# An output projection with the norm of its rows set between half products, and the next stage's first context product moved to its end

## The chip, the core and the metric

The kernel runs on one core of a Trainium2 chip. The metric is the device time of one execution in microseconds (us). The kernel's engines each follow a program of their own and meet at semaphores: TensorE (PE, with its weight loads as PEld), VectorE (DVE), ScalarE (ACT), GpSimd (POOL) and the sync engine (SP), which here only issues transfers.

## The reference, cut to what matters

The reference is a chain of two blocks in float32. The first ends in an attention layer, whose output is multiplied by `b_w_out`, gated and added to `x`. The second block starts with a layer (`layer = 0`) on the 1024 rows of `x` and on 256 context rows:

```python
h_lat = rms_norm(x_lat, norm1_g[layer]) * (1 + m_lat[1]) + m_lat[0]
h_ctx = rms_norm(x_ctx, norm1_g[layer]) * (1 + m_ctx[1]) + m_ctx[0]
...
z_lat = h_lat @ w_in
z_ctx = h_ctx @ (w_in if need_ctx else w_in[:, :EVEN_CTX_COLS])
...
q_ctx = z_ctx[..., EVEN_CTX_COLS:EVEN_CTX_COLS + A_Q_W].reshape(bsz, n_ctx, A_KV_HEADS, g, A_HEAD_DIM)
s_ctx = spatial_gating(z_ctx[..., EVEN_CTX_COLS + A_Q_W:], sgu_norm_g, sgu_w, sgu_b)
```

`w_in` is 1024 by 1792, and comes as four tiles of 1024 by 512 (the third padded): Q (the queries), V (the half of the gated part that is normed), K (keys and values) and U (the other half).

## The kernel before, in words

The kernel is a chain of stages (`block_...`). Each stage has one program for each engine; at its end all engines meet at a barrier. Activations stay in on-chip memory, as `X` (ten tiles of 128 rows by 1024, eight of `x` and two of the context) and `hT` (the normed rows, transposed, in eight pieces of 128 by 1280). Weights come from DRAM in tiles of 2 MB (`load_w`, issued by SP) into a ring of three slots. `slot_of` (L84) says which tile goes to which slot, and `next_tile` which tile is loaded into a slot once its present tile is used up. From the KV stage to the first layer's end only slots 1 and 0 hold weights; slot 2 holds sums of weights (`w_sums`).

**`block_out`** (L1886), as the stage `bout`, computes `x = x + gate * (attention output @ b_w_out)` and the transposed norm of all ten row tiles. TensorE's work is 16 half products: row tile i (0 to 7) by column half t (0, 1), each 8 matmuls of 128x512 (`product`, L399; the profile records each float32 matmul twice, so 16 records), into four PSUM banks (2 to 5) in turn. `gate_rows` (L1094) brings the gate into banks 6 and 7, once. For each half VectorE runs `residual_add` (L1236, L1238).

**`Follow`** (L265) is the norm. Its list of tiles is here `[8, 9, 0, ..., 7]`: the two context tiles come first (they are the `lead` of 2), so follow tile n holds row tile n-2. For each tile:

- ScalarE: `squares` (L285, sum of squares), then `normed` (root L298, scaled copy L302) into one of two buffers `xn`. `squares` of tile n writes into buffer n % 2 and so waits until tile n-2 has been transposed (`free`).
- VectorE: `dve_var` (L318) after the squares, `dve_rst` (L323) after the root.
- TensorE: `pe`, eight transposes (L351), four into bank 0 and four into bank 1. It waits for `normed` of this tile, and until both banks have been emptied of the tile before (`placed`).
- VectorE empties bank 0 (`dve_tile`, L332) and ScalarE bank 1 (`act_tile`, L311) into `hT`.

What sets the order is the list `turns`: after which row tile's products which follow tiles are transposed. It is `[[], [0], [1, 2], [3, 4], [5], [6], [7], [8]]`, and tile 9 comes after the loop. On VectorE `dve_tile` of `turns[i]` stands behind both `residual_add` of row tile i, and `dve_var(i + 2)`, which waits for ScalarE, stands behind that and ahead of the next `residual_add`.

SP loads the context rows (`in_ctx`, L1925) at the start, stores each finished row tile, and loads the next stage's tiles Q and V at the end (L1933 and L200).

**`block_ein`** (L2057) is the next stage. It starts with the products of the two context tiles by the Q tile (`rows_of_tile`, 16 matmuls of 128x512, into banks 0 and 1), which VectorE scales and copies (L2418). Then come 12 `Quads`, blocks of a product made with fewer multiplications, for which VectorE first makes sums of rows (`quad_sums`, L537 to L540, four times) and of weights (L522, L523, L529, L530). Quads 0 to 3 use tile Q, 4 to 7 tile V, 8 to 11 tile U. Each opens with two products (`pe_open`); the third waits for VectorE's `dve_11` (L482). At quad 4 the products of the context rows by the V tile are put in (16 matmuls again), and ScalarE's gelu of them. Then follow the K tile's products and the rest. VectorE makes the sums of row blocks 2 and 3 after the two copies of L2418.

Of the kernel before, what the change touches and what calls it, by code (L numbers as in the profile page):

```python
# [25 lines left out]
P = 128  # L26
# [58 lines left out]
def slot_of(n):  # L85
# [10 lines left out]
    own, one, two = [(2, 1, 0)[(k + j) % RING] for j in range(RING)]  # L96
# [1789 lines left out]
def block_out(cr, name, w0, nt, gates, tiles, col, router=None, homes=(A_OT, A_H), gated=None):  # L1886
# [28 lines left out]
    turns = [[], [0], [1, 2], [3, 4]] + [[i + 1] for i in range(4, nt)] if lead else [[i - 1] if i else [] for i in range(nt)]  # L1915
# [5 lines left out]
    with nc.Block() as block:  # L1921
        @block.sync
        def _(sp):
            if lead:
                sp.dma_start(Xr[:, NT:NTC], io["ctx"].rearrange("b (i p) d -> (b p) i d", p=P)).then_inc(x_in, 16)  # L1925
            if router is not None:
                sp.dma_start(rw, io["router"][:, router]).then_inc(r_in, 16)
            for i in range(nt):
                if i == nt - 1:
# [14 lines left out]
        def _(pe):  # L1944
# [12 lines left out]

            for i in range(nt):
# [10 lines left out]
                for n in turns[i]:  # L1969
                    fol.pe(pe, n)  # L1970
# [11 lines left out]
        def _(act):  # L1982
# [12 lines left out]
            for i in range(nt):  # L1995
                for n in turns[i]:
# [12 lines left out]
        def _(dve):  # L2009
# [7 lines left out]
            for i in range(nt):  # L2017
# [3 lines left out]
                for n in turns[i]:  # L2021
                    fol.dve_tile(dve, n)
# [9 lines left out]
def block_bout(cr):  # L2032
    block_out(cr, "bout", W_BOUT, NT, [(MC_B + 16, V_C)], [NT, NT + 1] + list(range(NT)), MC_L)
# [23 lines left out]
def block_ein(cr):  # L2057
# [23 lines left out]
    S, T = x_sums(cr), w_sums(cr)  # L2081
# [40 lines left out]
    with nc.Block() as block:  # L2122
        @block.sync
        def _(sp):
# [6 lines left out]
            sp.wait_ge(uc.full, 4 + NTC)  # L2131
# [32 lines left out]
        def _(pe):  # L2164
# [56 lines left out]
            cr.wait_w(pe, W_Q)  # L2221
            for i in (8, 9):
                rows_of_tile(cr.w(W_Q), i, 512)
# [21 lines left out]
        def _(act):  # L2245
# [19 lines left out]

            for n in range(9):
                if n < 8:
                    qd.act_1(act, n, blocks(n)[0])
                if n == 4:
                    for r in range(2):  # L2270
                        act.wait_ge(uc.full, 3 + r)
                        gelu(vr[:, 8 + r], uc.bank(2 + r)).then_inc(uc.empty, 1)
# [24 lines left out]
            act.wait_ge(uc.empty, 4 + NTC)  # L2297
            for m in range(4):
                act.wait_ge(uc.full, 4 + NTC + m + 1)
# [1338 lines left out]
```

## Time and profile before

| what | value |
|---|---|
| three runs | 4673.64, 4674.6, 4679.7 us, median 4674.6 us |
| the profiled execution | 4671.94 us, of which the span from the first to the last instruction is 4670.2 us |
| mean granted TensorE clock | 0.964 |
| stage `bout` | from 1430.8 to 1570.0 us of the span |
| stage `ein` | from 1570.9 to about 1822 us |
| TensorE busy | 4343.9 us, 93% of the span |

The span is cut into stages by their first instruction; times within it are microseconds from its start. A timeline row gives the start, the length, the engine, the line, the operation with its output and input, the count, and in brackets the engine's idle time before it with what ended it. Matmul records overlap a little (each runs on for a while after the next has started), so the pace is read from start to start. PEclk is the share of full clock granted.

### The profile page before, as it was taken

The numbers are of one execution on the slowest core, as the hardware profiler recorded it, in microseconds if no ns is written. First come the engines' busy times: TensorE is split into PE (matmuls) and PEld (weight loads), VectorE is DVE, ScalarE is ACT, GpSimd is POOL, SyncE is SP. The second block draws the span as 40 slices with busy tenths as digits, with TensorE's granted clock in tenths as the row PEclk, the third lists the DMA queues.
The fourth block names the chain that finished last, engine by engine and source line by source line (L and its number), as shares of the span: only waits on it lengthen the run. The fifth ranks groups of instructions, "written<-read, shape, count | busy, mean of one in ns | idle before, by whom it ended". The sixth has DMA issues, their size and how long they took to land. (4 is left out here: it accounts for less than half of the span.)

```text
span 4670.2 us, 63663 instructions
## 1 busy us (share of the span) xinstructions
PE 4343.9 (93%) x25960; PEld 3116.2 (67%) x25960; DVE 1648.0 (35%) x4208; ACT 1007.1 (22%) x2270; POOL 230.0 (5%) x281
## 2 busy tenths in 40 slices
PE   7996899999999999996999999989999995999996
PEld 3444446888664587643888888869656644888885
DVE  5408234433783344725111111133445524111111
ACT  2011122112663123722100000021135521000001
POOL 0100000000220000000000001000000000000000
PEclk8998999999999999997999999999999997999998
DMA  7668211223420112115677777741161013888887
GB/s 282 228 107 315 95 46 39 92 84 111 169 83 28 61 59 91 49 63 200 233 260 256 258 256 251 267 145 41 66 209 37 1 55 114 314 312 318 320 310 259
DMA packets 132953, 756.89 MB, mean 162 GB/s; under 512 B 13729, under 2 KB 52385, under 8 KB 97297
## 3 DMA queue, kind: packets, MB, share of 16 engines
q1 hardware_dynamic: 107248, 669.78, 39.1%
q0 software_dynamic: 20272, 64.76, 5.1%
q10 hardware_dynamic: 5232, 19.63, 1.2%
q8 instruction: 132, 2.16, 0.2%
q14 instruction: 69, 0.56, 0.0%
HBM read 663.46 MB, written 91.19 MB: 162 GB/s over the span
## 5 line engine op out<-in xcount | busy, mean ns | idle before, releaser
L2828 PEld LDWEIGHTS psum<-arena,w_ring 128*128 128x128 f32 x8192 | 1022.6, 192 | 15.5 <-issue 15.5
L2828 PE MATMUL psum<-arena,w_ring 128*128 128x160 f32 (+1 forms) x8192 | 1027.0, 288 | 4.5 <-ACT arena L2910 3.0
L399 PE MATMUL psum<-w_ring,arena 128*128 128x512 f32 (+3 forms) x1608 | 635.0, 553 | 13.0 <-PEq L194 9.6
L399 PEld LDWEIGHTS psum<-w_ring,arena 128*128 128x128 f32 x1608 | 305.0, 193 | 311.5 <-issue 282.4
L2843 PE MATMUL psum<-w_ring,arena 128*128 128x512 f32 x1024 | 450.0, 592 | 0.0
L427 PE MATMUL psum<-w_ring,arena 128*128 128x256 f32 (+1 forms) x2016 | 435.6, 377 | 15.3 <-PEq L194 7.1
L427 PEld LDWEIGHTS psum<-w_ring,arena 128*128 128x128 f32 x2016 | 377.8, 192 | 66.8 <-issue 17.6
L2969 DVE TENSOR_TENSOR arena<-arena,psum 128x320 f32<-128x320 f32 (+1 forms) x128 | 58.2, 455 | 956.9 <-PE psum L2828 956.9
L399 PE MATMUL psum<-arena,w_ring 128*128 128x512 f32 (+1 forms) x880 | 373.3, 580 | 2.8 <-DVE arena L332 1.6
L2894 ACT ACTIVATE arena<-psum 128x320 f32<-128x320 f32 (+1 forms) x128 | 52.5, 410 | 1311.0 <-PE psum L2828 1311.0
L2843 PEld LDWEIGHTS psum<-w_ring,arena 128*128 128x128 f32 x1024 | 189.7, 190 | 214.9 <-issue 214.9
L1683 PE MATMUL psum<-arena 64*128 64x256 f32 (+5 forms) x1056 | 319.8, 526 | 12.4 <-PEq L194 11.0
L427 PE MATMUL psum<-arena,w_ring 128*128 128x256 f32 x1344 | 295.7, 380 | 5.0 <-DVE arena L482 3.5
L399 PEld LDWEIGHTS psum<-arena,w_ring 128*128 128x128 f32 x880 | 165.5, 192 | 190.1 <-issue 186.2
L427 PEld LDWEIGHTS psum<-arena,w_ring 128*128 128x128 f32 x1344 | 253.4, 190 | 41.1 <-DVE w_ring L523 3.6
L1696 PEld LDWEIGHTS psum<-consts,arena 128*128 128x128 f32 x1552 | 172.9, 141 | 122.4 <-issue 68.7
L1733 ACT ACTIVATE arena<-psum 128x512 f32<-128x512 f32 (+3 forms) x436 | 194.2, 482 | 271.9 <-PE psum L1696 261.6
L1741 ACT ACTIVATE arena<-arena,small 128x640 f32<-128x640 f32 (+8 forms) x272 | 244.6, 900 | 6.0 <-DVE small L1788 5.9
L1696 PE MATMUL psum<-consts,arena 128*128 128x128 f32 x1552 | 224.0, 279 | 5.9 <-ACT arena L1741 4.5
L1713 PE MATMUL psum<-arena 128*64 128x128 f32 x3104 | 225.5, 281 | 0.0
L1683 PEld LDWEIGHTS psum<-arena 64*128 64x128 f32 (+1 forms) x1056 | 126.2, 191 | 100.4 <-issue 73.2
L1713 PEld LDWEIGHTS psum<-arena 128*64 128x64 f32 x3104 | 164.2, 136 | 42.5 <-issue 41.4
(378 smaller groups left out, 3427.4 us busy)
## 6 DMA issues: line engine op xcount, KB each, us to landing
w_ring<-in_wstream SPq DMA_DIRECT2D x258, 2048.0 KB, 7.8
x_rows<-arena SPq DMA_DIRECT2D x26, 512.0 KB, 2.7
w_ring<-in_wstream ACTq DMA_DIRECT2D x6, 2048.0 KB, 7.8
xn_rows<-arena POOLq DMA_DIRECT2D x18, 512.0 KB, 2.9
arena<-f_rows SPq DMA_DIRECT2D x8, 1024.0 KB, 7.6
arena<-x_rows SPq DMA_DIRECT2D x2, 4096.0 KB, 21.3
arena<-x_rows SPq DMA_DIRECT2D x8, 1024.0 KB, 9.5
arena<-in_x_first SPq DMA_DIRECT2D x4, 1024.0 KB, 21.9
```

The costliest lines, as they stand in the source:

```text
L399: last = cr.nc.tensor.matmul(bank_ap, l, r, start=(k == 0), stop=(k == len(pairs) - 1))
L427: last = self.cr.nc.tensor.matmul(out, l, r, start=(start and k == 0), stop=(k == len(pairs) - 1), skip_group_check=True)
L1683: nc.tensor.matmul(cr.bank[2 * h + C % 2][:, 0:p.b - p.a], s_.q(h), p.keys(h), start=True, stop=True).then_inc(qk, 1)
L1696: last = nc.tensor.transpose(cr.bank[4 + h][:, n * P:(n + 1) * P], s_buf[:, s % 3, h, col:col + P], cr.const(C_ID))
L1713: last = nc.tensor.matmul(o[h * HD:(h + 1) * HD], s_.pv[blk][1](h), t_buf[:, h, G % 2, n * P:(n + 1) * P], start=(blk == 0), stop=(blk == ...
L1733: copy = lambda to, of: nc.scalar.activation(to, of, ACT.Copy)
L1741: nc.scalar.activation(v, v, ACT.Exp, bias=shift_of(s, h), scale=-1.0, accum_out=rsum[:, s % 3, h:h + 1]).then_inc(pr, 1)
L2828: last = nc.tensor.matmul(half(bank0 + v)[:, c], w[:, k, m * P:(m + 1) * P], xT[:, k, :], start=(k == 0), stop=(k == KT - 1))
L2843: last = nc.tensor.matmul(cr.bank[YB[h]][:, :], hid[:, k, 0:CAP], w[:, k, :], start=(k == 0), stop=(k == KT - 1))
L2894: nc.scalar.activation(sa[:, v % 2], half(v % 2), ACT.Silu).then_inc(a_e, 1)
L2969: nc.vector.tensor_tensor(hid[:, 2 * v:2 * v + 2], sa[:, v % 2], half(2 + v % 2), ALU.mult).then_inc(b_e, 1)
```

## The change

It has four parts.

1. In `block_out`, `turns` now goes by half products: for `bout` tile 0 is transposed after half 2 (row tile 1, first half), tile 1 after half 3, tile 2 after half 4, tile 3 after half 5, tile 4 after half 7, and from there one tile after each second half, as before. VectorE's `dve_tile` stands at the same places. The other stages that use `block_out` keep their order.
2. The two products of context tiles by tile Q move from the start of `ein` to the end of `bout` (`following`): the first between the transposes of tiles 8 and 9, the second behind those of tile 9, into banks 6 and 7. VectorE's last act in `bout` is a wait for the second. In `ein` it copies from banks 6 and 7 without a wait.
3. In `ein` the products of the context rows by tile V move from quad 4 to the stage's start, and ScalarE's gelu of them with them. The unit numbers fall by two.
4. The ring: tile Q goes to slot 2 and is loaded at the start of `bout`, ahead of the context rows; in `ein` the weight sums are in slot 1; tile K goes to slot 2. Later tiles have slots 1 and 2 exchanged. The load of tile Q at the end of `bout` is gone; that of tile V stays.

```diff
@@ slot_of
+    if n < W_EIN:
+        return (1, 0)[(n - W_KV) % 2]
     if n < W_MOD2:
-        return (1, 0)[(n - W_KV) % 2]
+        return (2, 0)[(n - W_EIN) % 2]
     if n < W_OIN:
-        return (2, 1, 0)[(n - W_MOD2) % RING]
+        return (1, 2, 0)[(n - W_MOD2) % RING]
...
@@ block_out
-    turns = [[], [0], [1, 2], [3, 4]] + [[i + 1] for i in range(4, nt)] if lead else [[i - 1] if i else [] for i in range(nt)]
+    turns = {2: [0], 3: [1], 4: [2], 5: [3]} if lead else {3: [0], 5: [1]}
+    turns.update({2 * i + 1: [i - 1 + lead] for i in range(3, nt)})
+    of_half = lambda s: turns.get(s, ())
+    f_ok, = cr.sems(name, "following_rows")
...
         def _(sp):
+            if follower is not None:
+                cr.load_w(sp, follower)
             if lead:
                 sp.dma_start(Xr[:, NT:NTC], io["ctx"]...
...
-                if i == nt - 1:
+                if i == nt - 1 and follower is None:
                     sp.wait_ge(un.full, 2 * nt - 1)
                     cr.load_w(sp, cr.next_tile(w0))
...
+            def following(r):
+                w = cr.w(follower)
+                for k in range(KT):
+                    last = nc.tensor.matmul(cr.bank[6 + r][:, :], hT[:, k, (NT + r) * P:(NT + r + 1) * P], w[:, k, :], start=(k == 0), stop=(k == KT - 1))
+                return last
...
+            if follower is not None:
+                cr.wait_w(pe, follower)
+                pe.wait_ge(g_ok, 2)
+                following(0)
             fol.pe(pe, len(tiles) - 1)
+            if follower is not None:
+                following(1).then_inc(f_ok, 1)
...
             fol.dve_tile(dve, len(tiles) - 1)
+            if follower is not None:
+                dve.wait_ge(f_ok, 1)
@@ block_ein
-    S, T = x_sums(cr), w_sums(cr)
+    S, T = x_sums(cr), w_sums(cr, 1)
...
-                            if n == 4:
-                                for i in (8, 9):
-                                    rows_of_tile(cr.w(W_V), i, 512)
...
-            cr.wait_w(pe, W_Q)
+            cr.wait_w(pe, W_V)
             for i in (8, 9):
-                rows_of_tile(cr.w(W_Q), i, 512)
+                rows_of_tile(cr.w(W_V), i, 512)
             quads(0, 8)
...
+            for r in range(2):
+                act.wait_ge(uc.full, r + 1)
+                gelu(vr[:, 8 + r], uc.bank(r)).then_inc(uc.empty, 1)
...
             for r in range(2):
-                dve.wait_ge(uc.full, r + 1)
-                ts(rawq[:, 8 + r], uc.bank(r), HD ** -0.5, None, ALU.mult).then_inc(uc.empty, 1)
+                ts(rawq[:, 8 + r], cr.bank[6 + r][:, :], HD ** -0.5, None, ALU.mult)
```

The rows below are the program's order on an engine: a line number, the operation, output and input, shape, and a count. In the changed kernel the same helper stands two lines further down (L353 is L351, L401 is L399).

TensorE from the second half product of `bout` on, before:

```order
L399 MATMUL psum<-w_ring,arena 128x512 x24
L351 MATMUL psum<-consts,arena 128x128 x8
L399 MATMUL psum<-w_ring,arena 128x512 x16
L351 MATMUL psum<-consts,arena 128x128 x16
L399 MATMUL psum<-w_ring,arena 128x512 x16
L351 MATMUL psum<-consts,arena 128x128 x16
L399 MATMUL psum<-w_ring,arena 128x512 x16
```

and in the changed kernel:

```order
L401 MATMUL psum<-w_ring,arena 128x512 x16
L353 MATMUL psum<-consts,arena 128x128 x8
L401 MATMUL psum<-w_ring,arena 128x512 x8
L353 MATMUL psum<-consts,arena 128x128 x8
L401 MATMUL psum<-w_ring,arena 128x512 x8
L353 MATMUL psum<-consts,arena 128x128 x8
L401 MATMUL psum<-w_ring,arena 128x512 x8
L353 MATMUL psum<-consts,arena 128x128 x8
L401 MATMUL psum<-w_ring,arena 128x512 x16
```

Before, two tiles were transposed directly behind one another twice (the x16 of L351); now a half product (x8 of L401) stands between any two of the first four.

VectorE from `dve_var` of tile 2 on, before (L1236 and L1238 are a residual add, L332 empties bank 0):

```order
L318 TENSOR_SCALAR small<-small 128x1
L323 RECIPROCAL small<-small 128x1
L1236 TENSOR_TENSOR arena<-psum,arena 128x512
L1238 TENSOR_TENSOR arena<-arena 128x512
L1236 TENSOR_TENSOR arena<-psum,arena 128x512
L1238 TENSOR_TENSOR arena<-arena 128x512
L332 TENSOR_SCALAR arena<-psum,gs,modcol 128x128 x4
L318 TENSOR_SCALAR small<-small 128x1
L323 RECIPROCAL small<-small 128x1
```

and in the changed kernel:

```order
L320 TENSOR_SCALAR small<-small 128x1
L325 RECIPROCAL small<-small 128x1
L1238 TENSOR_TENSOR arena<-psum,arena 128x512
L1240 TENSOR_TENSOR arena<-arena 128x512
L334 TENSOR_SCALAR arena<-psum,gs,modcol 128x128 x4
L1238 TENSOR_TENSOR arena<-psum,arena 128x512
L1240 TENSOR_TENSOR arena<-arena 128x512
L334 TENSOR_SCALAR arena<-psum,gs,modcol 128x128 x4
L320 TENSOR_SCALAR small<-small 128x1
L325 RECIPROCAL small<-small 128x1
```

Tile 0 is now placed between the two residual adds of row tile 1, and tile 1 behind the second.

TensorE from the last two half products of `bout` to the first quads of `ein`, before (the branches are the stage boundary):

```order
L399 MATMUL psum<-w_ring,arena 128x512 x16
L351 MATMUL psum<-consts,arena 128x128 x16
L1921 UNCONDITIONAL_BRANCH
L2163 UNCONDITIONAL_BRANCH
L399 MATMUL psum<-w_ring,arena 128x512 x16
```

and in the changed kernel:

```order
L401 MATMUL psum<-w_ring,arena 128x512 x16
L353 MATMUL psum<-consts,arena 128x128 x8
L1969 MATMUL psum<-w_ring,arena 128x512 x8
L353 MATMUL psum<-consts,arena 128x128 x8
L1969 MATMUL psum<-w_ring,arena 128x512 x8
L1926 UNCONDITIONAL_BRANCH
L2185 UNCONDITIONAL_BRANCH
L401 MATMUL psum<-w_ring,arena 128x512 x16
```

The two products of L1969 now stand in `bout`; the x16 behind the boundary are by tile V instead of tile Q, and the x16 that stood at quad 4 are gone from there.

## Rows read from the trace of the kernel before

**Rows 1.** the page's first lines.

```profile
span 4670.2 us, 63663 instructions
```

**Rows 2.** TensorE in time, output and context stages (start, length, idle before and its releaser).

```profile
1430.85 7.11 PE L399 MATMUL psum<-w_ring,arena 128*128 128x512 f32 x16 [2.78 <-PEq L194]
...
1474.79 1.04 PE L351 MATMUL psum<-consts,arena 128*128 128x128 f32 x8
1481.89 1.94 PE L351 MATMUL psum<-consts,arena 128*128 128x128 f32 x8 [6.06 <-DVE arena L332]
1483.62 15.99 PE L399 MATMUL psum<-w_ring,arena 128*128 128x512 f32 x32
...
1502.57 1.06 PE L351 MATMUL psum<-consts,arena 128*128 128x128 f32 x8 [2.08 <-DVE arena L332]
...
1517.20 1.04 PE L351 MATMUL psum<-consts,arena 128*128 128x128 f32 x8
1518.07 13.90 PE L399 MATMUL psum<-w_ring,arena 128*128 128x512 f32 x32
...
1561.03 1.04 PE L351 MATMUL psum<-consts,arena 128*128 128x128 f32 x8
1566.50 1.97 PE L351 MATMUL psum<-consts,arena 128*128 128x128 f32 x8 [4.43 <-ACT arena L302]
1570.92 16.78 PE L399 MATMUL psum<-w_ring,arena 128*128 128x512 f32 x32 [2.45 <-PEq L194]
1587.53 3.62 PE L427 MATMUL psum<-w_ring,arena 128*128 128x256 f32 x16
```

**Rows 3.** granted TensorE clock (PEclk) in three stretches.

```profile
1481.90:1488.00 6.10, 6.10 (x14) 3.54 (x15) 1.69 (x6) 3.68 (x8) 0.00 (x0) 0.51 0.11 45
...
1570.90:1577.00 6.10, 6.08 (x8) 2.70 (x9) 5.95 (x8) 0.00 (x0) 0.00 (x0) 0.53 0.42 131
...
1594.20:1598.00 3.80, 3.79 (x11) 3.16 (x12) 2.22 (x2) 0.00 (x0) 0.00 (x0) 0.62 0.00 0
```

**Rows 4.** ScalarE and VectorE in time, output stage.

```profile
1440.75 1.06 ACT L285 ACTIVATE arena<-arena 128x1024 f32<-128x1024 f32 x1
...
1475.93 1.06 ACT L285 ACTIVATE arena<-arena 128x1024 f32<-128x1024 f32 x1 [10.27 <-PE psum L351]
...
1480.38 1.36 DVE L332 TENSOR_SCALAR arena<-psum,gs,modcol 128x128 f32<-128x128 f32 x4
```

**Rows 5.** the sync queue, ScalarE and VectorE in time, around the stage's end.

```profile
1563.12 0.42 SPq L200 DMA_DIRECT2D w_ring<-in_wstream  x1
...
1568.50 1.50 ACT L311 ACTIVATE arena<-psum,modcol,gs 128x128 f32<-128x128 f32 x4 [2.06 <-PE psum L351]
...
1593.65 0.42 DVE L482 TENSOR_TENSOR arena<-arena,psum 128x256 f32<-128x256 f32 x1
```

**Rows 6.** TensorE in time, inside the next stage.

```profile
1594.21 41.35 PE L427 MATMUL psum<-w_ring,arena 128*128 128x256 f32 x184 [3.06 <-DVE arena L482]
1635.40 13.90 PE L399 MATMUL psum<-w_ring,arena 128*128 128x512 f32 x32
1649.13 27.79 PE L427 MATMUL psum<-w_ring,arena 128*128 128x256 f32 x128
...
1773.10 41.68 PE L427 MATMUL psum<-arena,w_ring 128*128 128x256 f32 x192 [0.68 <-DVE arena L482]
...
1822.42 5.66 PE L1683 MATMUL psum<-arena 64*128 64x256 f32 x20 [3.45 <-PEq L194]
```

**Rows 7.** VectorE in time, the weight sums of the V tile.

```profile
1637.29 1.23 DVE L523 TENSOR_TENSOR w_ring<-w_ring 128x1024 f32<-128x1024 f32 x1
```

**Rows 8.** DMA issues over the whole span: size, median to landing.

```profile
arena<-x_rows SPq DMA_DIRECT2D x2, 4096.0 KB, 21.3
...
arena<-in_ctx SPq DMA_DIRECT2D x1, 1024.0 KB, 5.1
```

**Rows 9.** landing of the weight tiles loaded from the sync queue.

```profile
DMA to landing us min/median/max: 7.4/7.8/30.2
```

More of the change, by code:

```diff
@@ L90, in slot_of @@
         return (2, 0, 1)[(n - W_MOD1) % RING]
+    if n < W_EIN:
+        return (1, 0)[(n - W_KV) % 2]
     if n < W_MOD2:
-        return (1, 0)[(n - W_KV) % 2]
+        return (2, 0)[(n - W_EIN) % 2]
     if n < W_OIN:
-        return (2, 1, 0)[(n - W_MOD2) % RING]
+        return (1, 2, 0)[(n - W_MOD2) % RING]
     k = (W_OIN - W_MOD2) % RING
-    own, one, two = [(2, 1, 0)[(k + j) % RING] for j in range(RING)]
+    own, one, two = [(1, 2, 0)[(k + j) % RING] for j in range(RING)]
     if n < W_MOE1:
@@ L1883, with block_out @@
 A_H = 20480
-def block_out(cr, name, w0, nt, gates, tiles, col, router=None, homes=(A_OT, A_H), gated=None):
+def block_out(cr, name, w0, nt, gates, tiles, col, router=None, homes=(A_OT, A_H), gated=None, follower=None):
     nc, io = cr.nc, cr.io
@@ L1968, in _ @@
                         gate_rows(cr, diag[:, t], (6, 7), g_mm)
-                for n in turns[i]:
-                    fol.pe(pe, n)
+                    for n in of_half(2 * i + t):
+                        fol.pe(pe, n)
                 for g in range(len(groups)):
@@ L1995, in _ @@
             for i in range(nt):
-                for n in turns[i]:
+                for n in (*of_half(2 * i), *of_half(2 * i + 1)):
                     fol.act_tile(act, n)
@@ L2020, in _ @@
                                  Xr[:, i, t * 512:(t + 1) * 512], fol.fin if t else None)
-                for n in turns[i]:
-                    fol.dve_tile(dve, n)
+                    for n in of_half(2 * i + t):
+                        fol.dve_tile(dve, n)
                 fol.dve_var(dve, i + lead)
@@ L2032, in block_bout @@
 def block_bout(cr):
-    block_out(cr, "bout", W_BOUT, NT, [(MC_B + 16, V_C)], [NT, NT + 1] + list(range(NT)), MC_L)
+    block_out(cr, "bout", W_BOUT, NT, [(MC_B + 16, V_C)], [NT, NT + 1] + list(range(NT)), MC_L, follower=W_EIN)
 def variant(lat, ctx):
@@ L2130, in _ @@
             cr.load_w(sp, cr.next_tile(W_V))
-            sp.wait_ge(uc.full, 4 + NTC)
+            sp.wait_ge(uc.full, 2 + NTC)
             cr.load_w(sp, cr.next_tile(W_K))
@@ L2268, in _ @@
                     qd.act_1(act, n, blocks(n)[0])
[L2269 to L2272, printed above, removed]
                 if n:
@@ L2296, in _ @@
             act.wait_ge(placed, NQ)
-            act.wait_ge(uc.empty, 4 + NTC)
+            act.wait_ge(uc.empty, 2 + NTC)
             for m in range(4):
-                act.wait_ge(uc.full, 4 + NTC + m + 1)
-                gelu(uT[:, m, SEQ:NTOK], uc.bank(4 + NTC + m)[:, 0:256]).then_inc(uc.empty, 1)
+                act.wait_ge(uc.full, 2 + NTC + m + 1)
+                gelu(uT[:, m, SEQ:NTOK], uc.bank(2 + NTC + m)[:, 0:256]).then_inc(uc.empty, 1)
             for n in range(8, 13):
@@ L2350, in rows_kv @@
             def rows_kv(i):
-                u = 4 + i
+                u = 2 + i
                 dve.wait_ge(uc.full, u + 1)
@@ L2382, in moments @@
                     else:
-                        dve.wait_ge(uc.empty, 3 + r)
+                        dve.wait_ge(uc.empty, 1 + r)
                     ln(nc.vector.bn_stats(bn6, vr[:, ROWS[r]]))
@@ L2480, in _ @@
                 if n == 8:
-                    dve.wait_ge(uc.full, 4 + NTC + 4)
+                    dve.wait_ge(uc.full, 2 + NTC + 4)
                     sums_34(2)
@@ L2486, in _ @@
                     dve.wait_ge(s_mx, 10)
[L2487 removed]
+                    dve.wait_ge(uc.empty, 2 + NTC + 4)
                     u = uT[:, :, SEQ:NTOK].rearrange("p g (i c) -> p g i c", c=P)
```

1 line of the change is left out of this document (removed).

## The prediction

> **What bounds the kernel now.** I read the page's head first: a span of 4670.2 us [rows 1], with TensorE busy nearly all of it. A stage is therefore worth what TensorE loses in it, and I next read TensorE in time through the two stages that the change touches, looking only at the brackets (idle time and its releaser) and at starts that come later than the pace allows. The pace is 6.87 us for a half product and 0.87 us for a tile's eight transposes: from 1517.20 to 1518.07 are the transposes, and 32 records (two half products) from 1635.40 to 1649.13 take 13.73 us [rows 2, 6]. Against that pace TensorE loses time at four places.
>
> - Before tile 2's transposes it waits 6.06 us for L332 on VectorE, and then works slowly: 1.94 us where the next tiles take 1.04, and 15.99 us where 32 records else take 13.90 [rows 2]. The granted clock there is 0.51, the lower level of 1.2 GHz [rows 3].
> - Before tile 4's transposes it waits 2.08 us, again for L332 [rows 2]. The transposes behind it take 1.06 us, so the clock did not fall.
> - At the end of `bout` it waits 4.43 us for the scaled copy of tile 9, transposes slowly, waits 2.45 us for the stage boundary and runs the first products of `ein` at half clock: 16.78 us for 32 records [rows 2], clock 0.53 [rows 3].
> - Inside quad 0 it waits 3.06 us for `dve_11` on VectorE [rows 6], and the clock is 0.62 in the 3.8 us behind [rows 3].
>
> Then I read ScalarE and VectorE for why. The first loss is a chain: ScalarE's squares of tile 3 need the buffer of tile 1, which is transposed only after half 5, so they start at 1475.93 after 10.27 us of idling; VectorE's `dve_var` stands behind them and ahead of the residual adds of row tile 2, and `dve_tile(1)`, for which TensorE waits, starts only at 1480.38 [rows 4]. The last loss is VectorE's order: the row sums of blocks 2 and 3 stand behind the copy of the second Q product, so `dve_11` runs at 1593.65 [rows 5], 6.1 us after the quads started at 1587.53 [rows 2].
>
> **The order by half products.** The amount of work does not change. Does a new wait come in place of the old? With a half product between any two of the first four tiles, whatever stands between two transposes has 6.87 us. The longest of these is the chain that cost 6.06 us: from the start of squares to the end of the L332 group is 1480.38 + 1.36 - 1475.93 = 5.81 us with two residual adds in it [rows 4]. Now one add stands there. It fits, with over a microsecond to spare even at its old length. Tile 1, behind half 3, is the tightest: VectorE is held in `dve_var(2)` until the squares of tile 2 have run, and those start only when tile 0 is transposed; behind it come one add and one L332, so the old 5.81 us is again the bound. From tile 4 on the order is the old one, but tile 3 is now out of the way a half product or more earlier, so the 2.08 us go as well. Gain: 6.06 + (1.94 - 1.04) + (15.99 - 13.90) + 2.08 = 11.1 us. Bounds: at least 6.06 + 2.08 - 3 = 5 if one such wait of a few microseconds stays, at most 11.1, since nothing else is lost there. I take 11.1.
>
> **The load at the start.** Tile Q (2 MB) is issued ahead of the context rows. These landed in 5.1 us alone, and a tile takes 7.8 in the median [rows 8, 9]: landing in turn they come after about 13 us, near 1444, where the squares started at 1440.75 [rows 4]. So ScalarE and VectorE start some 3 us late, and the first residual adds too. The cover is TensorE's: it needs tile 0's copy after half 2 (1430.85 plus gate and three halves, about 1453) and an emptied bank only for half 4. Cost 0; without that cover it would be 3 us. The Trainium skill, DMA: Bandwidth & Descriptors, section Queues, rings and completion order, says that on each DMA engine the descriptors of one issuing queue are taken in ring order. That speaks against this edit, since the context rows then can't overtake the tile. No row of this trace has the two in flight together. By that rule the rows come at about 1444, without it up to 8 us earlier; the sum is the same, the rule only makes the late-context rival below possible.
>
> **The end of `bout` and the start of `ein`.** Before: from the transposes of tile 8 (1561.03) to the first quad (1587.53) are 26.50 us [rows 2], and the V products of the context rows at quad 4 are 13.73 us more [rows 6]: 40.2 us. After: transposes 0.87, first Q product 6.87, transposes 0.87, second Q product 6.87, the boundary, V products 13.73. Tile 9's copy was ready 1566.50 - 1561.03 = 5.47 us after half 15's end; the transposes of tile 8 and the first product last 7.7, so that wait is gone. The placing of tile 9 (ScalarE's L311 ends at 1568.50 + 1.50, 3.5 us after its transposes began [rows 2, 5]) hides behind the second product. The boundary took 0.92 us from ScalarE's end at 1570.00 to 1570.92; there is now a hop from TensorE to VectorE's added wait ahead of it, behind which only the barrier is queued. Bounds 0.9 and 3.45 us, the longest idle of TensorE at a boundary here [rows 6]; I take 1.2, as it is near the same boundary's row. Sum: 29.2 + 1.2 = 30.4. Gain 40.2 - 30.4 = 9.8 us. Tile V is still issued about 2 us after half 15's end (1563.12 before [rows 5]) and is needed 16.7 us after it; alone in the queue it lands in 7.8, so it costs nothing. Tile Q has been there for 100 us.
>
> **Quad 0.** VectorE's copies no longer wait, so all its sums are made while TensorE is at the V products. What is left is the bare reply of `dve_11`, 0.68 us at quad 8 [rows 6]. Gain 3.06 - 0.68 = 2.4 us. The clock falls no more: 184 records took 41.35 us where 192 took 41.68 [rows 6], so at that pace 184 take 39.94. Gain 1.4 us. Bounds of both: 2.4 to 3.8 in all.
>
> **Quad 4.** The V products covered VectorE's sums of tile V, which ended at 1637.29 + 1.23, 3.1 us after the products began at 1635.40 [rows 6, 7]. Now quad 4's two opening products (3.62 us in quad 0 [rows 2]) and a third product stand there before the first sum is needed: the cover is shorter by a half but holds. ScalarE's gelu moves to a place where it has nothing else; it ends before quad 0's first copy. Cost 0, at most 1 us. The exchanged slots move no transfer after `ein` and cost 0.
>
> **Sum.** 11.1 + 9.8 + 2.4 + 1.4 = 24.7 us. The profiled execution took 4671.9 us, so 4647.2; the median shown is 2.7 us above that execution, by which it would be 4649.9. I take 4648. All later stages wait for this chain, so they start earlier by the same amount.
>
> **Rivals.**
>
> - *The wait moves to the new order.* VectorE is in `dve_var(2)` while TensorE is at half 3, and each later pair inherits the lag. For it: VectorE serves both the norm and the residual adds. Against: 5.81 against 6.87 us. Then the 11.1 us are mostly kept in new places and 13.6 remain: 4658.
> - *The boundary is dear.* TensorE is now the last engine, and its end, VectorE's wait and the barrier follow each other. At 3.45 us instead of 1.2, with the first products slow again (16.78 - 13.90 = 2.9), 5.1 are lost: 4653. For it: after idle times of 6.06, 4.43 and 3.06 us the clock fell. Against: after 2.78 and 2.08 it did not, 7.11 us for 16 records and 1.06 for eight transposes [rows 2]. The Trainium skill, TensorE: Matmul & The Clock Gate, section What's actually happening, has the clock halved by inactivity and given back after sustained work. The trace agrees; by the rule a boundary of 1.2 us costs no clock.
> - *The gain isn't there.* Context products in `bout` and V products at the front only change places while TensorE stays as busy, and some later wait eats the rest: within 9 us of before, 4667. Against: the losses are idle time in front of named waits.
> - *Slower: the context rows come late.* All hangs on the copy of tile 0, for TensorE stands behind it after half 2. If the tile takes its maximum of 30.2 us and the 1 MB behind it as long as 4 MB elsewhere, 21.3 [rows 8, 9], squares start at 1482.7 and the transposes about 4 us later, 33 us after 1453: 33 - 24.7 = 8 slower, or with 3 us of half clock 11: 4683. It decides from a landing after about 1474 on (where the stall exceeds the gain), 43 us after issue. Against: no other transfer is in flight there.
>
> **How the numbers follow.** Forecast 0.74 (its own range 4643 to 4652), new wait 0.10, dear boundary 0.11, no gain 0.03, late context 0.02. The range that leaves 2 in 10 outside reaches up to the first two rivals, 4641 to 4657; downward it has only the boundary and the spread between executions. A measurement of this kernel can tell 0.2%, 9.3 us, from no change: faster holds the forecast and the first two rivals, 0.95; same 0.03; slower 0.02.
>
> **What would show it.** In the profile after: no bracket over 1 us on TensorE between the first half product of `bout` and its end, and 13.9 us for each pair; full clock there; the stage's last half product ending near 1549.9; L1969's two products 7.7 us apart start to start; about 1.2 us before `ein`; under 1 us before `dve_11` of quad 0; nothing new at quad 4. A wait at an L353 group for VectorE would prove the first rival, a granted clock near 0.5 in the first 6 us of `ein` the second.

## The result and the profile after

The changed kernel took 4646.93 us in the median (4642.45 to 4656.39, 4 runs), the kernel before, on the same chip, 4676.12 us (4 runs). The ratio is 0.9948, 95% interval 0.9936 to 0.996. Two later comparisons gave 0.995 (0.9936 to 0.9963) and 0.9944 (0.9931 to 0.9958). As a gain the three ratios are 24.3, 23.4 and 26.2 us, where 24.7 were forecast. The difference of the first two medians, 29.2 us, is larger, but still inside the interval of the first ratio (18.7 to 29.9 us). The profiled execution shows less: it took 4656.39 us, the slowest of its four, on a span of 4654.6 us, which is 15.6 us under the span before. Why a profile can show 15.6 us where the ratio shows 24.3 is itself something to learn here, so I first compare the two stages by their own length.

TensorE in time in the changed kernel, the output stage and the start of the next (start, length, idle before; L353 are transposes, L401 half products and then the V products, L1969 the Q products, L429 the quads; a group that goes on past the end of a view is shown with the records up to there):

```profile
1437.68 8.80 PE L401 MATMUL psum<-w_ring,arena 128*128 128x512 f32 x16 [2.78 <-PEq L196]
...
1461.84 1.04 PE L353 MATMUL psum<-consts,arena 128*128 128x128 f32 x8
1462.71 7.03 PE L401 MATMUL psum<-w_ring,arena 128*128 128x512 f32 x16
...
1485.07 1.04 PE L353 MATMUL psum<-consts,arena 128*128 128x128 f32 x8
1485.94 13.90 PE L401 MATMUL psum<-w_ring,arena 128*128 128x512 f32 x32
...
1558.12 1.04 PE L353 MATMUL psum<-consts,arena 128*128 128x128 f32 x8
1558.99 7.03 PE L1969 MATMUL psum<-w_ring,arena 128*128 128x512 f32 x16
1565.86 1.04 PE L353 MATMUL psum<-consts,arena 128*128 128x128 f32 x8
1566.73 7.03 PE L1969 MATMUL psum<-w_ring,arena 128*128 128x512 f32 x16
1574.92 13.97 PE L401 MATMUL psum<-w_ring,arena 128*128 128x512 f32 x32 [1.16 <-PEq L196]
1588.73 3.62 PE L429 MATMUL psum<-w_ring,arena 128*128 128x256 f32 x16
```

The reader is to see three things against [rows 2]. No L353 row has a bracket, nor has any in the lines left out: the waits of 6.06, 2.08 and 4.43 us are gone. Every pair of half products (32 records) takes 13.90 us, also the one behind tile 3, and a single one between two tiles 7.03. The stage boundary is 1.16 us. The same view further on:

```profile
1593.03 67.58 PE L429 MATMUL psum<-w_ring,arena 128*128 128x256 f32 x312 [0.68 <-DVE arena L484]
...
1686.97 3.72 PE L429 MATMUL psum<-w_ring,arena 128*128 128x256 f32 x16 [1.72 <-ACT arena L473]
...
1756.77 41.68 PE L429 MATMUL psum<-arena,w_ring 128*128 128x256 f32 x192 [0.67 <-DVE arena L484]
...
1806.09 5.32 PE L1685 MATMUL psum<-arena 64*128 64x256 f32 x20 [3.45 <-PEq L196]
```

From quad 0's second part the 312 records run in one piece of 67.58 us, with no V products among them; before, the same 312 were two pieces of 41.35 and 27.79 us [rows 6]. The wait ahead of them is 0.68 us, as at quad 8. VectorE's copies of the Q products no longer wait in `ein`. Before, the second copy waited 6.10 us for TensorE, with the sums of blocks 2 and 3 behind it:

```profile
1587.73 0.69 DVE L2418 TENSOR_SCALAR arena<-psum 128x512 f32<-128x512 f32 x1 [6.10 <-PE psum L399]
```

and in the changed kernel, the last sum and `dve_11`:

```profile
1589.00 0.68 DVE L542 TENSOR_TENSOR arena<-arena 128x512 f32<-128x512 f32 x1
1592.46 0.42 DVE L484 TENSOR_TENSOR arena<-arena,psum 128x256 f32<-128x256 f32 x1 [2.77 <-PE psum L429]
```

Now VectorE waits for TensorE, 2.77 us, and not the other way round.

The account, from start to start, in us (the window stage is the one behind `ein`; its first matmul is L1685):

| stretch | before | after | gain | forecast |
|---|---|---|---|---|
| first half product to the end of the 16th | 130.18 | 120.44 | 9.7 | 11.1 |
| from there to quad 0 (before with the 13.73 at quad 4) | 40.23 | 30.61 | 9.6 | 9.8 |
| quad 0, to its second part | 6.68 | 4.30 | 2.4 | 2.4 |
| clock behind it | 68.82 | 67.41 | 1.4 | 1.4 |
| from there to the first matmul of the window stage | 145.66 | 145.65 | 0.0 | 0 |
| sum | 391.57 | 368.41 | 23.2 | 24.7 |

The first line holds a loss of 1.7 us that the change does not cause. The very first half product of `bout` took 8.80 us instead of 7.11. The view by stretches shows it (PEclk, the granted clock, is the figure behind the brackets; DMA share and GB/s follow):

```profile
1437.60:1446.30 8.70, 8.62 (x16) 3.74 (x17) 1.66 (x8) 0.00 (x0) 0.00 (x0) 0.80 0.88 327
1446.30:1558.10 111.80, 111.80 (x321) 53.95 (x320) 33.84 (x80) 35.91 (x71) 0.00 (x0) 1.00 0.09 36
1574.90:1581.00 6.10, 6.08 (x14) 2.75 (x15) 5.94 (x8) 1.26 (x1) 0.00 (x0) 1.00 0.43 131
```

The clock was 0.80 over the first half product and 1.00 from there to the end of the sixteenth; in the first 6 us of `ein`, where 0.53 stood [rows 3], it is 1.00. Without those 1.7 us the first line would gain 11.4.

What lies outside the two stages: ahead of them this profile has 1437.68 us where before had 1430.85, 6.8 us more, and behind them 2848.5 against 2847.8. The code ahead is the same. So of the 23.2 us of the two stages 6.8 and 0.7 are lost outside them in this pair of profiles, which leaves the 15.6. Executions without a profile have no times by stage.

### The profile page after: what moved, and what is told of

It reads as the page before. It is cut to its first block and busy times, and to the rows that moved or that the text cites. A ratio compares the mean times of both kernels' runs of the same rounds, so it can differ in the third digit from the quotient of the medians.

```text
span 4654.6 us, 63706 instructions
## 1 busy us (share of the span) xinstructions
PE 4342.8 (93%) x25960; PEld 3110.1 (67%) x25960; DVE 1647.6 (35%) x4208; ACT 1008.1 (22%) x2270; POOL 230.5 (5%) x281
## 5 line engine op out<-in xcount | busy, mean ns | idle before, releaser
L401 PE MATMUL psum<-w_ring,arena 128*128 128x512 f32 (+3 forms) x1576 | 619.1, 550 | 11.7 <-PEq L196 8.3
L401 PEld LDWEIGHTS psum<-w_ring,arena 128*128 128x128 f32 x1576 | 297.5, 192 | 301.2 <-issue 272.5
L429 PE MATMUL psum<-w_ring,arena 128*128 128x256 f32 (+1 forms) x2016 | 435.3, 376 | 13.5 <-PEq L196 7.1
L429 PEld LDWEIGHTS psum<-w_ring,arena 128*128 128x128 f32 x2016 | 377.7, 192 | 64.7 <-issue 15.6
L401 PE MATMUL psum<-arena,w_ring 128*128 128x512 f32 (+1 forms) x880 | 376.0, 583 | 2.8 <-DVE arena L334 1.7
L1685 PE MATMUL psum<-arena 64*128 64x256 f32 (+5 forms) x1056 | 319.7, 526 | 12.3 <-PEq L196 10.6
L429 PE MATMUL psum<-arena,w_ring 128*128 128x256 f32 x1344 | 297.3, 381 | 5.0 <-DVE arena L484 3.5
L401 PEld LDWEIGHTS psum<-arena,w_ring 128*128 128x128 f32 x880 | 166.4, 193 | 191.8 <-issue 188.8
L429 PEld LDWEIGHTS psum<-arena,w_ring 128*128 128x128 f32 x1344 | 254.6, 191 | 41.6 <-DVE w_ring L525 3.6
L1685 PEld LDWEIGHTS psum<-arena 64*128 64x128 f32 (+1 forms) x1056 | 126.2, 190 | 100.6 <-issue 73.7
```

Of the source, the lines that this page charges most:

```text
L401: last = cr.nc.tensor.matmul(bank_ap, l, r, start=(k == 0), stop=(k == len(pairs) - 1))
L429: last = self.cr.nc.tensor.matmul(out, l, r, start=(start and k == 0), stop=(k == len(pairs) - 1), skip_group_check=True)
L1685: nc.tensor.matmul(cr.bank[2 * h + C % 2][:, 0:p.b - p.a], s_.q(h), p.keys(h), start=True, stop=True).then_inc(qk, 1)
```

## The experiments

Each run below has a profile; the table gives for each the start of `bout` (its first half product), the length of that half product, the length L from it to the first matmul of the window stage, L with the first half product taken at 7.10 us, and the ratio to the kernel before.

| kernel | start | first half product | L | L at 7.10 | ratio (95% interval) |
|---|---|---|---|---|---|
| before | 1430.85 | 7.11 | 391.57 | 391.6 | |
| changed | 1437.68 | 8.80 | 368.41 | 366.7 | 0.9948 (0.9936 to 0.996) |
| e9_after_again | 1436.35 | 8.59 | 368.20 | 366.7 | 0.995 (0.9936 to 0.9963) |
| e9_third | 1430.43 | 10.17 | 369.78 | 366.7 | 0.9944 (0.9931 to 0.9958) |
| e1_order | 1435.32 | 8.80 | 378.84 | 377.1 | 0.9974 (0.9962 to 0.9985) |
| e2_follow | 1428.79 | 8.53 | 379.13 | 377.7 | 0.9966 (0.9952 to 0.9979) |
| e3_ctx_first | 1429.66 | 8.54 | 368.15 | 366.7 | 0.9943 (0.9929 to 0.9957) |
| e4_ctx_late | 1428.40 | 8.58 | 400.27 | 398.8 | 1.0018 (1.0009 to 1.0027) |
| e5_sums_first | 1431.35 | 7.11 | 387.77 | 387.8 | 0.9991 (0.9982 to 1.0) |
| e6_v_at_quad4 | 1428.57 | 7.10 | 380.10 | 380.1 | 0.9977 (0.9968 to 0.9987) |
| e7_both_behind | 1431.87 | 7.10 | 373.62 | 373.6 | 0.9961 (0.9946 to 0.9976) |
| e8_one_root | 1433.96 | 7.10 | 365.46 | 365.5 | 0.9941 (0.9928 to 0.9955) |

### The changed kernel again, twice

No edit.

> The changed kernel once more, unchanged, to learn which part of the measured gain (4676.12 to 4646.93 us, 29.2 us) repeats. Theory (the waits in the two stages are the whole cause): from the first half product of bout to the first matmul of the window stage 366.7 to 368.5 us again, where the kernel before took 391.6 us, the difference of 1.7 us being whether the first half product runs at half clock; and whatever is above 25 us in the medians is spread between executions of the stages ahead of bout. Rival (the exchanged slots or the earlier load also help elsewhere): the gain of the medians stays near 29 us and stages outside these two are shorter in the profile, each time.

> The changed kernel a third time, for one more profile of the stages ahead of bout and one more comparison with the kernel before. Theory (what is above 25 us is spread): the stages ahead of bout take another time again, and the ratio stays within its interval. Rival: they take the same as in the first profile.

Measured: medians 4650.8 us (before 4674.54) and 4647.89 us (before 4673.77). L at 7.10 is 366.7 us in all three profiles, so the two stages repeat to a tenth. (The 391.6 of the kernel before is from one profile; e5_sums_first has the same code up to quad 0 and takes the same 156.68 us for it.) Behind them the three profiles have 2848.5, 2848.0 and 2846.5 us. Ahead of them they have 1437.68, 1436.35 and 1430.43 us, a spread of 7 us in the same code. Over all twelve profiles here that start lies between 1428.4 and 1437.7, without regard to the kernel. So the theory holds: the change is worth 24.9 us in its stretch (391.6 - 366.7), and nothing in the profiles speaks for more; the 29.2 us of the first medians did not come again (medians 23.7 and 25.9 us apart). In the third profile the first half product was slow beyond what I had allowed (10.17 us, 3.1 above the fast one), so that L itself, 369.78 us, lies above the 368.5 that I expected.

### The order alone, and the moved products alone

```diff
 kernel before, bout only:
-    turns = [[], [0], [1, 2], [3, 4], [5], [6], [7], [8]]      by row tile
+    turns = {2: [0], 3: [1], 4: [2], 5: [3], 7: [4], 9: [5], ...}   by half product
 and fol.pe / dve_tile at those places; nothing else of the change
```

> The kernel before with the order by half products alone (turns and dve_tile); everything else as before. Theory: the waits of 6.06 and 2.08 us and the half clock behind the first go, the end of bout and quad 0 stay: 11.1 to 11.4 us less than before, near 4664. First half product to the end of the sixteenth: 118.8 us, or up to 1.7 more if the first runs at half clock, where before took 130.2. Rival (VectorE's lag in the variance of tile 2 is passed on, and the gain needs the other edits): a new wait for L332's group in front of a tile's transposes and under 6 us gain.

Measured: 4662.08 us, ratio 0.9974, which is 12.2 us. TensorE in time, the first tiles and the end:

```profile
1435.32 8.80 PE L399 MATMUL psum<-w_ring,arena 128*128 128x512 f32 x16 [2.77 <-PEq L194]
...
1459.48 1.04 PE L351 MATMUL psum<-consts,arena 128*128 128x128 f32 x8
...
1467.22 1.04 PE L351 MATMUL psum<-consts,arena 128*128 128x128 f32 x8
...
1474.96 1.04 PE L351 MATMUL psum<-consts,arena 128*128 128x128 f32 x8
...
1561.22 1.50 PE L351 MATMUL psum<-consts,arena 128*128 128x128 f32 x8 [4.43 <-ACT arena L302]
1565.18 15.66 PE L399 MATMUL psum<-w_ring,arena 128*128 128x512 f32 x32 [2.45 <-PEq L194]
...
1587.36 39.95 PE L427 MATMUL psum<-w_ring,arena 128*128 128x256 f32 x184 [3.06 <-DVE arena L482]
```

No bracket in front of the first four transposes: the order needs nothing from the other edits. The waits of 4.43 and 3.06 us are still there. L is 12.7 us shorter. Taken apart: 11.4 for the two waits and the clock behind the first, -1.7 for the slow first half product, and 1.6 and 1.4 because the clock fell less behind the 4.43 us (1.50 us for the transposes, before 1.97, and 15.66 us for 32 records, before 16.78) and not at all behind the 3.06 us (39.95 us for 184 records, before 41.35). These two are the same waits as before with another reply of the clock, and no part of what the order gains.

```diff
 changed kernel:
-    turns = {2: [0], 3: [1], 4: [2], 5: [3]}
+    turns = {3: [0], 5: [1, 2], 7: [3, 4]}
 ...                                     tile 5 after half 9, and on as before
```

> The changed kernel with the old order of the norm (tile 0 after half 3, tiles 1 and 2 after half 5, 3 and 4 after half 7), so the moved products and the slots alone. Theory (the parts add up): 9.8 us at the stage's end, 2.4 + 1.4 at quad 0, in all 13.6 us less than before, near 4661; the 6.1 and 2.1 us waits are there again. Rival (the early load of tile Q is paid for by late context rows, hidden in the new order only): the first transposes wait, and gain under 11 us.

Measured: 4657.72 us, ratio 0.9966, 15.9 us (interval 9.8 to 22.4). L at 7.10 is 13.9 us shorter than before. In its profile the transposes of tiles 2 and 4 wait again:

```profile
1481.25 1.94 PE L353 MATMUL psum<-consts,arena 128*128 128x128 f32 x8 [6.06 <-DVE arena L334]
...
1501.47 1.07 PE L353 MATMUL psum<-consts,arena 128*128 128x128 f32 x8 [2.08 <-DVE arena L334]
...
1576.74 13.97 PE L401 MATMUL psum<-w_ring,arena 128*128 128x512 f32 x32 [1.16 <-PEq L196]
...
1594.85 5.42 PE L429 MATMUL psum<-w_ring,arena 128*128 128x256 f32 x24 [0.68 <-DVE arena L484]
```

The first transposes have no bracket (the rival expected a wait there).

The parts add up, once the clock is set aside. By L at 7.10, before rounding, e1_order saves 14.4 us and e2_follow 13.9, together 28.3 where the whole is 24.9. Of these, 3.5 us are the clock's: the 1.6 and 1.4 above, and in e2_follow 0.45, as the 32 records behind the 6.06 us took 15.54 us where they took 15.99 before. What is left is 11.4 for the order and 13.4 for the moved products (9.6 + 3.8, as in the account), 24.8 in all.

### The context rows first, and the context rows late

```diff
 changed kernel, sync engine in bout:
-            cr.load_w(sp, follower)
             sp.dma_start(Xr[:, NT:NTC], io["ctx"]...).then_inc(x_in, 16)
+            cr.load_w(sp, follower)
```

> The changed kernel with the context rows loaded ahead of tile Q instead of behind it. In the changed kernel the rows landed 9.7 us after issue. Theory (the landing is hidden by the gate's copies and by the slack up to half 2): the rows land in about 5 us, and nothing on TensorE moves: within 2 us of the changed kernel. Rival (the squares start late and hold up the first residual adds): squares start earlier and the time falls by 2 to 3 us.

Measured: L at 7.10 is 366.7, the same as the changed kernel's to a tenth; 4644.83 us against its 4650.8 in the same comparison, which is inside the spread of starts (1429.66 against 1436.35). The rows landed 4.9 us after issue instead of 9.7. The first squares (L287) of both, each preceded by ScalarE's copies of the gate (L2011), context rows first and then the changed kernel:

```profile
1440.02 1.09 ACT L2011 ACTIVATE arena<-psum 128x512 f32<-128x512 f32 x2 [12.71 <-PE psum L1096]
1440.99 1.06 ACT L287 ACTIVATE arena<-arena 128x1024 f32<-128x1024 f32 x1
```

```profile
1448.31 1.09 ACT L2011 ACTIVATE arena<-psum 128x512 f32<-128x512 f32 x2 [12.97 <-PE psum L1096]
1449.28 1.06 ACT L287 ACTIVATE arena<-arena 128x1024 f32<-128x1024 f32 x1
```

Both start 0.97 us behind the start of the gate copies: ScalarE was not waiting for the rows in either. But in the profile of the changed kernel the slow first half product had held the gate back by 1.7 us. Where the first half product ran fast and the rows came behind the tile, the rows came last, as in e8_one_root:

```profile
1442.89 1.08 ACT L2011 ACTIVATE arena<-psum 128x512 f32<-128x512 f32 x2 [11.27 <-PE psum L1096]
1444.22 1.06 ACT L287 ACTIVATE arena<-arena 128x1024 f32<-128x1024 f32 x1 [0.24 <-DMA arena<-in_ctx]
```

Here it is 1.33 us, in e6_v_at_quad4 1.09 and in e7_both_behind 1.22. So the squares start up to 0.4 us late, and TensorE's slack hides it: none of the three has a bracket at tile 0's transposes.

```diff
 changed kernel, sync engine in bout:
+                for m in range(5):
+                    sp.dma_start(cr.ring[:, SLOT[follower], :], io["wstream"][follower]).then_inc(again, 16)
+                    sp.wait_ge(again, 16 * (m + 1))
                 cr.load_w(sp, follower)
             sp.dma_start(Xr[:, NT:NTC], io["ctx"]...)
```

> The changed kernel with tile Q loaded six times over, one after the other (each waited for on the sync queue), ahead of the context rows; the data are the same. Theory (TensorE stands behind the copy of tile 0 after half 2, so a landing later than about 22 us after the stage's start costs its full excess): five extra loads of about 8.3 us each put the landing at 50 to 54 us after the start, TensorE idles 32 to 38 us in front of tile 0's transposes, then some 3 us for tile 1 and 3 us of half clock: 36 to 44 us more than the changed kernel, which is 8 to 20 us slower than before. Rival (TensorE can go on with half products whatever the norm does): under 10 us more.

Measured: 4680.44 us, ratio 1.0018 (1.0009 to 1.0027), 8.4 us slower than before. TensorE:

```profile
1482.86 1.97 PE L353 MATMUL psum<-consts,arena 128*128 128x128 f32 x8 [30.35 <-ACT arena L304]
1484.62 7.72 PE L401 MATMUL psum<-w_ring,arena 128*128 128x512 f32 x16
1492.18 1.04 PE L353 MATMUL psum<-consts,arena 128*128 128x128 f32 x8
```

and the landing of the context rows, issued at 1468.9:

```profile
DMA to landing us min/median/max: 9.8/9.8/9.8
```

The rows landed 50.3 us after the stage's start; TensorE waits 30.35 us for tile 0's copy. L is 32.1 us more than the changed kernel's, somewhat below the 36 to 44 that I expected: there is no second wait at tile 1, and the half clock cost 1.6 us, not 3. The rival (TensorE goes on regardless) falls. Worked out from this one run, an estimate: a landing up to 20 us after the start (50.3 - 30.35) costs nothing, and if each further microsecond is paid in full and the clock costs 1.6 us, the change would be even with the kernel before at about 43 us. No run has a landing between 10.6 and 50.3 us.

### Quad 0

```diff
 kernel before, VectorE in ein:
+            row_sums(2)
+            row_sums(3)
             for r in range(2):
                 dve.wait_ge(uc.full, r + 1)
                 ts(rawq[:, 8 + r], uc.bank(r), ...)
-            row_sums(2)
-            row_sums(3)
```

> The kernel before with VectorE's row sums of blocks 2 and 3 ahead of the two copies of the Q products instead of behind them. Theory (the 3.06 us wait in quad 0 is VectorE's order alone): the wait falls to about 0.7 us and the half clock behind it goes: 2.4 + 1.4 = 3.8 us less than before, without any product moved. Rival (the wait is for the copies of the Q products, which come after the second product in either case): 0.69 us of the copy still stands before dve_11, nothing else; the wait is then 0.7 to 1.1 us and the gain still 3.3 or more; if the gain is under 1 us, the wait was of another cause.

Measured: 4668.53 us, ratio 0.9991 (0.9982 to 1.0). The interval of the ratio reaches to no change, but the stretch resolves it: L is 3.80 us shorter.

```profile
1588.03 3.62 PE L427 MATMUL psum<-w_ring,arena 128*128 128x256 f32 x16
1592.33 39.95 PE L427 MATMUL psum<-w_ring,arena 128*128 128x256 f32 x184 [0.68 <-DVE arena L482]
```

The wait is 0.68 us and 184 records take 39.95 us, at the pace that I had read from quad 8 (39.94). So the 3.06 us wait came from VectorE's sums standing behind copies that wait for TensorE. This run takes the sums out from behind the copies; the changed kernel leaves them there and takes the copies' wait away. Either gives the 3.8 us, so they could have been had without any product moved.

```diff
 changed kernel, TensorE in ein (and ScalarE's gelu with it):
-            for i in (8, 9):
-                rows_of_tile(cr.w(W_V), i, 512)
             quads(0, 8)
 and the same two products behind wait_w at n == 4
```

> The changed kernel with the V products of the context rows left at quad 4, so that ein starts with quad 0 directly. Theory (they stand at the front as cover for VectorE's sums): quad 0 opens at once, in 3.6 us, and then waits for VectorE, whose sums and copies take some 14 us from the stage's start: an idle time of 9 to 11 us, half clock behind it for about 1.5 us, so 10 to 12 us more than the changed kernel. Rival (the place of the V products does not matter, only the number of matmuls): within 2 us of the changed kernel.

Measured: 4662.46 us, ratio 0.9977; L is 13.4 us above the changed kernel's at 7.10, more than the 10 to 12 that I expected.

```profile
1564.11 3.69 PE L429 MATMUL psum<-w_ring,arena 128*128 128x256 f32 x16 [1.16 <-PEq L196]
1579.35 22.85 PE L429 MATMUL psum<-w_ring,arena 128*128 128x256 f32 x93 [11.55 <-DVE arena L484]
```

TensorE opens quad 0 at once and then idles 11.55 us, while VectorE works, mostly at sums, from the stage's first instruction to 1578.78 + 0.41:

```profile
1564.11 0.69 DVE L539 TENSOR_TENSOR arena<-arena 128x512 f32<-128x512 f32 x1 [7.05 <-PEq L196]
...
1578.78 0.41 DVE L484 TENSOR_TENSOR arena<-arena,psum 128x256 f32<-128x256 f32 x1
```

The V products at the front are therefore not a change of place for its own sake: without them the Q products moved into `bout` would have left VectorE's 15 us of work bare but for quad 0's opening. Of the 13.4 us, 10.9 are the wait (11.55 - 0.68) and 2.5 the clock behind it, a microsecond more than I had put.

### Both Q products behind tile 9

```diff
 changed kernel, TensorE at the end of bout:
-            following(0)
             fol.pe(pe, len(tiles) - 1)
+            following(0)
             following(1)
```

> The changed kernel with both Q products behind the transposes of tile 9 instead of one between tiles 8 and 9. Theory (the product between them fills the wait for tile 9's copy): the wait of 4.4 us for the scaled copy is back in front of the last transposes, and half clock behind it costs 0.9 us at the transposes and 2 to 3 at the product: 7 to 8.5 us more than the changed kernel. Rival (the gain at the end comes from the boundary having work on both sides, not from the filled wait): under 5 us more.

Measured: 4653.23 us, ratio 0.9961; L is 6.9 us above the changed kernel's at 7.10.

```profile
1550.60 1.04 PE L353 MATMUL psum<-consts,arena 128*128 128x128 f32 x8
1556.27 1.94 PE L353 MATMUL psum<-consts,arena 128*128 128x128 f32 x8 [4.63 <-ACT arena L304]
1558.01 15.16 PE L1969 MATMUL psum<-w_ring,arena 128*128 128x512 f32 x32
```

The wait is back with 4.63 us, and half clock behind it (1.94 us for the transposes, 15.16 for the two products instead of 13.90). That is 0.1 us below my lower bound; the rival's "under 5" falls. Of the 9.6 us at the stage's end, 6.9 are the product between tiles 8 and 9. The other 2.7, which this run keeps, are 1.3 of the boundary (2.45 to 1.16 us) and 1.6 of the clock, which behind the wait cost the products 1.3 us here and 2.9 before, less 0.2 because the wait was longer here. Why the clock cost less is open.

### The first root behind the last gelu

```diff
 changed kernel, ScalarE in ein:
                 if n < 8:
                     qd.act_2(act, n, blocks(n)[1])
-                if n == 7:
-                    root(0)
...
+            root(0)
             root(1)
```

> The changed kernel with ScalarE's first root (of the spatial gate's norm) moved from quad 7 behind the last gelu of quad 7. In quad 8's place TensorE waits 1.72 us for ScalarE, behind a root whose table load is followed by a second table load for the gelu. Theory (two of the three table loads of 1.28 us there are of the root's making): both go ahead of the last third-stage copy, the wait of 1.72 us falls to about 0.5 us, and the stage from bout's first half product to the window stage is 1.2 us shorter; in the medians it can't be told from the changed kernel. Rival (the norms come later for it and hold up the mixing products): waits of the mixing products for ScalarE or VectorE appear and the gain is lost.

Measured: 4646.02 us against 4647.89 for the changed kernel in the same comparison, ratio to before 0.9941 (0.9928 to 0.9955). TensorE's wait of 1.72 us:

```profile
1680.31 3.72 PE L429 MATMUL psum<-w_ring,arena 128*128 128x256 f32 x16 [0.47 <-ACT arena L473]
```

L is 365.5 us, 1.2 us less than the changed kernel's, as expected, and no wait came in its place. The changed kernel's ScalarE loads a table of 1.28 us three times there, at 1680.29 for the root, at 1684.20 for the gelu and at 1692.56 for the root again; here only one load is left, at 1685.89. It is the shortest version in the profiled stretch; in whole executions it can't be told from the changed kernel.

## Why the prediction was right

**The order by half products** (11.1): 11.4 at equal clock, and no wait came in its place, as e1_order shows alone. The argument that a chain of 5.81 us fits behind a half product of 6.87 held: in the changed kernel, from the squares of tile 2 (1462.98) to the end of the L334 group of tile 0 (1466.10 + 1.37) it took 4.5 us, and TensorE wanted the bank only at 1469.58. I undercounted by 0.3, since a bracket leaves out the tail of the record before it: from start to start tile 2's transposes came 7.10 us after tile 1's, 6.23 above the pace, where the bracket says 6.06.

**The load at the start** (0): right, with a wrong size in it. The rows did come behind the tile (2.5 us after it in the changed kernel's profile), as the prediction took it from the order of one queue. But they landed in 9.7 us, not in the 13 that I added up from single transfers, so the squares started up to 0.4 us late and not 3. e4_ctx_late bears out the slow rival's place, and roughly its price: it was to decide from 43 us after issue, and the estimate from that run is about 43. e3_ctx_first shows that nothing of it is paid here.

**The end of `bout` and start of `ein`** (9.8): 9.6. The boundary was 1.16 us where I took 1.2; the other 0.2 us are again the tail of the record before a bracket, and the V products, which took 13.97 us and not 13.90. The rival of a dear boundary did not happen: the clock in the first 6 us of `ein` was 1.00.

**Quad 0** (3.8): 3.8, as the copies wait no more. One detail was off: the last sum ended at 1589.68, 1 us after quad 0 opened, so the V products alone did not cover the sums; quad 0's opening products covered the rest.

**Quad 4** (0): 0. No bracket between 1593.03 and 1660.44.

**The number.** The stretch bears out the sum, 24.9 us against 24.7, with a term 0.3 too small and one 0.2 too large. That the first ratio gives 24.3 is closer than it could be relied on to be, with an interval of 18.7 to 29.9 us.

**What was wrong in it.** One reading: I used "after 2.78 us of idling the clock did not fall" [rows 2] as a fact of that wait. It is not one. The same idle time at the same place was followed by a slow first half product in seven of the twelve profiles. The forecast "full clock there" failed for that one half product, which cost this profile 1.7 us and e9_third 3.1. It is not the change: e1_order, with the old load order, has it, and e6, e7 and e8, with the new one, don't. The sum was not moved by it, but a single profile compared with another is. The sign "last half product ending near 1549.9" failed as well, at 1558.1: 6.8 us are the later start, 1.7 this clock, less the 0.3 undercounted.

## What to carry to other kernels

Where a norm or a transposition is threaded between matmuls, write down the longest chain between two of its steps and compare it with the unit of cover; one unit between every two steps did here what two units between every second pair did not. When work is moved across a stage boundary to fill a wait, ask what it covered where it stood: here VectorE's sums and copies needed 15 us of cover at the front of `ein`, and other products had to take the place. Judge a local change by the length of its own stretch in the profile, and set aside a slow first group that the change did not make: so taken it repeated here to 0.1 us, where whole executions of the changed kernel differed by up to 14.

## What the runs showed of the hardware

- The granted clock does not follow from the length of an idle time alone. Idle for 2.78 us ahead of `bout`, TensorE then ran the first half product in 7.10 to 7.11 us in five profiles and in 8.53 to 10.17 us in seven. Two of them, by 3 us stretches (the 2.8 us of idling, then the first and second 3 us of work), e6_v_at_quad4 and e9_third:

```profile
1425.77:1428.57 2.80, 0.02 (x3) 0.04 (x1) 0.43 (x2) 0.38 (x1) 0.72 (x1) 1.00 0.00 0
1428.57:1431.57 3.00, 3.00 (x7) 1.40 (x8) 1.65 (x8) 0.00 (x0) 0.00 (x0) 1.00 0.74 191
1431.57:1434.57 3.00, 3.00 (x8) 1.33 (x7) 0.00 (x0) 0.00 (x0) 0.00 (x0) 1.00 0.99 426
```

```profile
1427.63:1430.43 2.80, 0.03 (x2) 0.03 (x1) 0.43 (x1) 0.38 (x1) 0.72 (x1) 0.89 0.00 0
1430.43:1433.43 3.00, 3.00 (x4) 1.45 (x5) 1.66 (x8) 0.00 (x0) 0.00 (x0) 0.50 0.76 197
1433.43:1436.43 3.00, 3.00 (x4) 1.04 (x4) 0.00 (x0) 0.00 (x0) 0.00 (x0) 0.50 0.97 415
```

  Work before, idling and work after are alike in the two; PEclk is 1.00 throughout in the one, and 0.89, 0.50, 0.50 in the other. Likewise 3.06 us of idling was followed by a fallen clock in the kernel before (0.62 [rows 3]) and by a full one in e1_order (1.00). What decides it these runs don't show. The Trainium skill, TensorE: Matmul & The Clock Gate, section What's actually happening, calls the number of slow matmuls at a kernel's start variable from run to run; the runs here show the same in the middle of a kernel, with 7.10 to 10.17 us for the same 16 records.
- Two transfers issued 0.4 us apart from the sync queue did not take the sum of their single times: 1 MB landed 9.7 to 10.2 us after issue behind 2 MB, where ahead of it or alone it took 4.9 to 5.1 and the 2 MB 7.8 in the median, in sum 12.7 to 12.9. In the other order (e3_ctx_first) the 2 MB landed 9.3 us after issue. Added single times were 2.5 to 3 us too long for the two in a row.
- Ahead of the changed stages the same instructions took between 1428.4 and 1437.7 us in the twelve profiles.
